# First expert's rows by one-hot products on chip, in a two-layer decoder kernel

## The reference

```python
def hierarchical_moe(h, w_group, b_group, w_router, b_router, w_gate, w_up, w_down):
    hf = h.reshape(b * t, d)                       # 512 x 1024
    grp_p = softmax(hf @ w_group + b_group)        # 4 groups, the best one is taken
    g_sel = argmax(grp_p); g_w = grp_p[g_sel]
    exp_logits = (hf @ w_router + b_router)[g_sel] # 4 experts in the group
    top_p, top_i = top_k(softmax(exp_logits), 2)   # the best two of them
    weights = g_w * top_p / sum(top_p)
    ...
    for e in range(16):
        act = silu(hf @ w_gate[e]) * (hf @ w_up[e])      # 1024 -> 512
        y = y + combine[:, e:e + 1] * (act @ w_down[e])  # 512 -> 1024
    return y
```

## Time and profile before

| | us |
|---|---|
| median of 3 runs | 1290.84 (1289.98 to 1293.81) |
| the profiled execution, its own time | 1289.33 |
| its span in the trace | 1287.6 |
| PE busy (MATMUL) | 1168.3, 91% of the span |
| DVE busy | 912.4, 71% |
| ACT busy | 672.9, 52% |
| POOL busy | 94.5, 7% |
| DMA | 282.52 MB, mean 219 GB/s |

### The profile page before, as it was taken

How to read it: one execution, slowest core, us unless ns; L and a number is a source line. 1 busy time by engine, 2 the same in 40 slices (tenths; PEclk the granted TensorE clock), 3 DMA queues, 4 the chain that set the end, 5 groups by cost and what they waited for, 6 DMA issues and landing times.

```text
span 1287.6 us, 16726 instructions
## 1 busy us (share of the span) xinstructions
PE 1168.3 (91%) x5676; PEld 886.6 (69%) x5676; DVE 912.4 (71%) x1243; ACT 672.9 (52%) x843; POOL 94.5 (7%) x132
## 2 busy tenths in 40 slices
PE   5999879999769999999978999998957999999995
PEld 4776559878647767666646688887855766667663
DVE  4646658555578888888866247646566988888886
ACT  4335641133337787777743241132424787788771
POOL 1120000000010000000030000001001000000003
PEclk9999999899879999999989999999978999999998
DMA  6231110113489999999960240113177999999965
GB/s 221 90 88 66 66 66 1 66 66 132 161 307 354 387 388 385 381 384 391 370 216 1 70 133 18 66 66 131 66 260 258 382 381 380 391 385 384 381 234 206
DMA packets 129645, 282.52 MB, mean 219 GB/s; under 512 B 18976, under 2 KB 19488, under 8 KB 129584
## 3 DMA queue, kind: packets, MB, share of 16 engines
q1 hardware_dynamic: 119680, 246.98, 52.9%
q0 software_dynamic: 6112, 21.76, 5.4%
q10 hardware_dynamic: 3792, 12.98, 2.6%
HBM read 262.83 MB, written 18.87 MB: 219 GB/s over the span
## 4 chain that ended last, share of the span: by engine, by line
PE 57%; DVE 23%; issue 10%; ACT 6%; DMA 2%; POOL 1%; DVEq 1%; ACTq 0%; SPq 0%; POOLq 0%
PE PS L1104 16%; PE PS L1106 16%; PE PS L1105 15%; DVE expert_w_low L1815 9%; PE PS L1208 4%; DVE group_low L1599 2%; ACT weight_high L865 1%; DMA xg<-h_rows,idx 1%; PE PS L1143 1%; DVE xgT_low L1823 1%; DVE score_max L1730 1%; DVE act L1836 1%; DVE x_sb L1534 1%; PE PS L1318 1%; DVE hT_low L1583 1%
## 5 line engine op out<-in xcount | busy, mean ns | idle before, releaser
L1815 DVE TENSOR_TENSOR expert_w_low<-expert_w,weight_high 128x1024 fp32r<-128x1024 f32 x368 | 426.3, 1220 | 74.1 <-ACT weight_high L865 71.8
L865 ACT ACTIVATE weight_high<-expert_w 128x1024 fp32r<-128x1024 f32 x384 | 374.9, 1048 | 65.1 <-PE PS L1106 57.3
L1104 PE MATMUL PS<-weight_high,xgT_high 128*96 128x512 f32 x512 | 204.5, 399 | 7.1 <-DVEq L1825 4.1
L1106 PE MATMUL PS<-weight_high,xgT_low 128*96 128x512 f32 x512 | 203.2, 397 | 0.0
L1105 PE MATMUL PS<-expert_w_low,xgT_high 128*96 128x512 f32 x512 | 202.1, 395 | 0.0
L1104 PE MATMUL PS<-group_high,hT_high 128*128 128x512 f32 x416 | 173.3, 417 | 13.6 <-DVEq L1586 9.2
L1106 PE MATMUL PS<-group_high,hT_low 128*128 128x512 f32 x416 | 166.2, 399 | 0.0
L1105 PE MATMUL PS<-group_low,hT_high 128*128 128x512 f32 x416 | 165.9, 399 | 0.0
L1104 PE MATMUL PS<-weight_high,actT_high 128*96 128x512 f32 x256 | 104.4, 408 | 9.4 <-DVEq L1850 9.0
L1104 PEld LDWEIGHTS PS<-weight_high,xgT_high 128*96 128x96 f32 x512 | 83.3, 163 | 41.8 <-DVEq L1825 4.6
L1599 DVE TENSOR_TENSOR group_low<-group_w,group_high 128x1024 fp32r<-128x1024 f32 x68 | 80.7, 1222 | 43.3 <-ACT group_high L889 39.5
(11 more groups left out here) (248 smaller groups left out, 1436.2 us busy)
## 6 DMA issues: line engine op xcount, KB each, us to landing
expert_w<-in_moe_w_gate SPq DMA_DIRECT2D x32, 2048.0 KB, 13.9
expert_w<-in_moe_w_up SPq DMA_DIRECT2D x32, 2048.0 KB, 14.7
expert_w<-in_moe_w_down SPq DMA_DIRECT2D x32, 2048.0 KB, 13.4
group_w<-in_even_w_in SPq DMA_DIRECT2D x6, 2048.0 KB, 7.8
group_w<-in_odd_w_in SPq DMA_DIRECT2D x6, 2048.0 KB, 7.9
y_rows<-yb ACTq DMA_DIRECT2D x30, 384.0 KB, 6.1
group_w<-in_even_w_out SPq DMA_DIRECT2D x2, 2048.0 KB, 7.9
h_rows<-h SPq DMA_DIRECT2D x8, 512.0 KB, 11.1
```

What stands on the lines that cost most here:

```text
L865: act_(hi, w, ACT.Copy).then_inc(w_hi, 1)
L1104: pe.matmul(out, ah, bh, start=first, stop=False)
L1106: return pe.matmul(out, al, bh, start=False, stop=final)
L1815: tt(lo, w, hi.bitcast(F32), ALU.subtract).then_inc(w_lo, 1)
```

## The change

Expert 0's rows are no longer gathered. DVE makes four more one-hot tiles `oh0` (128 tokens x 96 places, zero where a token doesn't go to expert 0) in the memory of `ein`, and PE multiplies the normalised rows `h`, which are in SBUF, with them: 8 x 4 products of 128x128 by 128x96 in float32, right behind the index product. They give the transposed rows in banks 4 and 5 at once. POOL's first gather takes expert 1's rows. On the other engines the order follows:

- SP: the load of expert 2's gate weights, over `h`, waits for the new product too.
- ACT: `rows_T(0)`, `silu(0)`, half of `high(GATE)`, `rows_T(1)`, the other half, `lastT`.
- PE: `rows_T(1)` is in the middle of expert 0's up product, `lastT` behind it.
- DVE: the copy of `idx` and `nx`, `off` come before `rows_T(0)`, `first_low(1)` behind it as a whole, then q, b, j and the last `ohj`, `low(GATE)` in halves around `rows_T(1)`. `slot` is worked out at the end of block 0 (`slots`), `eid` at the end of block 13 (`further`).

```diff
--- before
+++ after
@@ -365,6 +365,8 @@
             w_of=[2, NT], w_last=[NT], ein=[16, NE],
             ein2=[16, NE], eidf=[16],
         ).items():
+            if name == "ein":
+                oh0 = at("first_onehot", [P, NT, CAP], F32, cursor[0])
             rt[name] = sb("r_" + name, [P] + shape)
         slot = sb("slot", [P, 2, NT], I32)
         assert cursor[0] <= nc.sbuf_usable_end
@@ -413,6 +415,7 @@
         r_gl, r_eg, r_x2, r_e2 = sem("r_groups"), sem("r_exp_groups"), sem("r_second"), sem("r_exp_second")
         M_ready, oh_ready, idx_ready, eid_ready = sem("assigned"), sem("onehots"), sem("idx_ready"), sem("eid_ready")
         idxcol_ready, gathered = sem("idxcol_ready"), sem("gathered")
+        oh0_ready = sem("first_onehot_ready")
         xgT_ready, ex_ready = sem("xgT_ready"), sem("gate_silu_ready")
         xgTh_ready, actTh_ready = sem("xgT_high_ready"), sem("actT_high_ready")
         w_hi, w_lo, w_lo_first = sem("weight_high_ready"), sem("weight_low_ready"), sem("first_low_ready")
@@ -672,6 +675,7 @@
                 expert("up", 1, 4)
                 sp.wait_ge(h_stored, 16 * NT * (l + 1))
                 bk.wait_full(sp, ("route", l))
+                bk.wait_full(sp, ("xgT", l))
                 expert("gate", 2, 5)
 
                 def block_loads(b, par, before="down"):
@@ -791,12 +795,12 @@
                 pool.wait_ge(idx_ready, l + 1)
                 pool.wait_ge(h_stored, 16 * NT * (l + 1))
                 pool.sem_inc(gather_issued, 1)
-                pool.indirect_dma_start(xg[0:CAP, :], None, hbuf[l][:], bass.IndirectOffsetOnAxis(idx[:, 0:1], 0)
+                pool.indirect_dma_start(xg[0:CAP, :], None, hbuf[l][:], bass.IndirectOffsetOnAxis(idx[:, 1:2], 0)
                                         ).then_inc(gathered, 16)
-                with pool.Fori(1, NE) as b:
+                with pool.Fori(2, NE) as b:
 
                     bk.wait_full(pool, ("xgT", l), b - 1)
-                    gather(l, b, idxcol_ready, b + l * (NE - 1), gathered)
+                    gather(l, b, idxcol_ready, b + (l * (NE - 2) - 1), gathered)
                 pool.wait_ge(eid_ready, l + 1)
                 more = pool.value_load(eid[0:1, 15:16], min_val=0, max_val=NX)
                 pool.wait_ge(zero_stored, 16 * NL)
@@ -857,10 +861,10 @@
 
             load_norm(0)
             for l in range(NL):
-                def high(p0, b=0, par=0):
+                def high(p0, b=0, par=0, which=range(SPLITS)):
 
                     wait_loaded(sc, l, p0, b, par)
-                    for part in range(SPLITS):
+                    for part in which:
                         w, hi, _ = parts(l, p0, par, part)
                         act_(hi, w, ACT.Copy).then_inc(w_hi, 1)
 
@@ -1059,14 +1063,14 @@
                         high(LAST)
 
                 rows_T(0, 0)
+                silu(0)
+                high(GATE, which=range(0, 2))
                 rows_T(1, 1)
+                high(GATE, which=range(2, SPLITS))
                 key = ("lastT", l)
                 bk.wait_full(sc, key)
                 link(act_(lastT[:], bank(key)[0:CAP], ACT.Copy))
                 sc.sem_inc(bk.freed(key), 1)
-                bk.wait_full(sc, ("gate", l))
-                high(GATE)
-                silu(0)
                 expert_loop(sc, block_act, link)
                 sc.wait_ge(eid_ready, l + 1)
                 more = sc.value_load(eid[0:1, 15:16], min_val=0, max_val=NX)
@@ -1338,6 +1342,16 @@
                     ins = pe.matmul(bank(key)[0:CAP, 0:NE], ohj[:, k], rt["tok"][:, c, i], start=k == 0, stop=k == 2 * NT - 1)
                 ins.then_inc(bk.filled(key), 1)
 
+                key = ("xgT", l)
+                pe.wait_ge(h_ready, NT * (2 * l + 2))
+                pe.wait_ge(oh0_ready, l + 1)
+                bk.acquire_in_loop(pe, key, 0)
+                for c in range(KD):
+                    for i in range(NT):
+                        ins = pe.matmul(PS[:, 4 + c // 4, c % 4 * CAP:(c % 4 + 1) * CAP], h[:, i, c * P:(c + 1) * P],
+                                        oh0[:, i], start=i == 0, stop=i == NT - 1)
+                ins.then_inc(bk.filled(key), 1)
+
 
                 def wait_low(pos, b, part):
                     if pos < 2:
@@ -1347,7 +1361,7 @@
 
                 def rows_T(b):
                     key = ("xgT", l)
-                    pe.wait_ge(gathered, b * 16 + 16 * (l * NE + 1))
+                    pe.wait_ge(gathered, b * 16 + 16 * l * (NE - 1))
                     bk.acquire_in_loop(pe, key, b)
                     for c in range(KD):
                         ins = pe.transpose(PS[:, 4 + c // 4, c % 4 * CAP:(c % 4 + 1) * CAP],
@@ -1404,17 +1418,15 @@
                     if not last:
                         into("up", b + 1, 1 - par, UP, b, par)
 
-                rows_T(0)
                 pe.wait_ge(xgT_ready, l * NE + 1)
                 into("gate", 0, 0, 0, 0, 0)
-                rows_T(1)
+                into("up", 0, 0, 1, 0, 0, lambda: rows_T(1))
                 key = ("lastT", l)
                 pe.wait_ge(last_ready, l + 1)
                 bk.acquire(pe, key)
                 for i in range(NT):
                     ins = pe.transpose(bank(key)[0:CAP, i * P:(i + 1) * P], ohj[:, i], ident[:])
                 ins.then_inc(bk.filled(key), 1)
-                into("up", 0, 0, 1, 0, 0)
                 expert_loop(pe, block_pe)
                 pe.wait_ge(eid_ready, l + 1)
                 more = pe.value_load(eid[0:1, 15:16], min_val=0, max_val=NX)
@@ -1799,14 +1811,10 @@
                     link(tt(ohj[:, c * NT:(c + 1) * NT], iota_f[:, 0:CAP].unsqueeze(1).broadcast_to(shape),
                             r["rk"][:, c].unsqueeze(2).broadcast_to(shape), ALU.is_equal))
                     ve.sem_inc(oh_ready, 1)
-                first_low(1, range(0, 2))
-                key = ("idx", l)
-                bk.wait_full(ve, key)
-                link(cp(idx[:, 0:NE], bank(key)[0:CAP, 0:NE]))
-                ve.sem_inc(idx_ready, 1)
-                ve.sem_inc(bk.freed(key), 1)
-                first_low(1, range(2, SPLITS))
-
+                for i in range(NT):
+                    ins = ts(oh0[:, i], iota_f[:, 0:CAP], rank[:, i, 0:1], r["M"][:, i, 0:1], ALU.is_equal, ALU.mult)
+                link(ins)
+                ve.sem_inc(oh0_ready, 1)
                 def low(p0, b=0, par=0, which=range(SPLITS)):
 
                     for part in which:
@@ -1836,6 +1844,29 @@
                     link(tt(act[0:CAP], bank(("up", l))[0:CAP], ex[0:CAP], ALU.mult))
                     ve.sem_inc(act_ready, 1)
                     ve.sem_inc(bk.freed(("up", l)), 1)
+
+                def slots():
+
+                    for of, by in (("bc", "b"), ("jc", "j")):
+                        link(tt(r["tA"], r["OH"], r[by].unsqueeze(1).broadcast_to(both), ALU.mult))
+                        link(red(r[of], r["tA"], AX, ALU.add))
+                    link(stt(r["jz"], r["bc"], float(NE - 1), r["jc"], ALU.not_equal, ALU.mult))
+                    link(stt(r["sl"], r["bc"], float(CAP), r["jz"], ALU.mult, ALU.add))
+                    link(cp(slot[:], r["sl"]))
+
+                def further():
+
+                    it8 = iota_f[:, 0:16].unsqueeze(2).broadcast_to([P, 16, NE])
+                    off8 = r["off"].unsqueeze(1).broadcast_to([P, 16, NE])
+                    nx8 = r["nx"].unsqueeze(1).broadcast_to([P, 16, NE])
+                    link(tt(r["ein"], it8, off8, ALU.subtract))
+                    link(tt(r["ein2"], r["ein"], nx8, ALU.is_lt))
+                    link(stt(r["ein2"], r["ein"], 0.0, r["ein2"], ALU.is_ge, ALU.mult))
+                    link(tt(r["ein2"], r["ein2"], iota_f[:, 0:NE].unsqueeze(1).broadcast_to([P, 16, NE]), ALU.mult))
+                    link(red(r["eidf"], r["ein2"], AX, ALU.add))
+                    link(red(r["eidf"][:, 15:16], r["nx"], AX, ALU.add))
+                    link(cp(eid[:], r["eidf"]))
+                    ve.sem_inc(eid_ready, 1)
 
                 def block_ve(b, par):
 
@@ -1860,6 +1891,10 @@
                         times_up(b + 1)
                     if is_int and b == NE - 2:
                         low(LAST, which=range(SPLITS - 1, SPLITS))
+                    if is_int and b == 0:
+                        slots()
+                    if is_int and b == NE - 3:
+                        further()
 
                 ve.wait_ge(r_eg, l + 1)
                 link(red(r["gsum"], r["eg"], AX, ALU.add))
@@ -1870,16 +1905,18 @@
                 link(tt(r["wt"][:, 1], r["wt"][:, 0], r["e2"], ALU.mult))
                 link(tt(r["w_of"], r["OH"][:, :, :, NE - 1], r["wt"], ALU.mult))
                 link(tt(r["w_last"], r["w_of"][:, 0], r["w_of"][:, 1], ALU.add))
-                for i in range(NT):
-                    ins = ts(ohj[:, i], iota_f[:, 0:CAP], rank[:, i, NE - 1:NE], r["M"][:, i, NE - 1:NE], ALU.is_equal, ALU.mult)
-                link(ins)
-                ve.sem_inc(last_ready, 1)
-
```

(35 more changed lines are left out.)

## The result

Over 20 runs of each, the changed kernel takes 1295.07 us in the median (1292.95 to 1297.34) and the one before 1289.20 (1285.17 to 1293.81): ratio 1.0049, 95% interval [1.0041, 1.0057], slower. The one of the changed kernel is 2.2 us above its median, near the top of its 20.

What follows compares the result with a forecast made beforehand. PE was taken as the main bound, with DVE level with it in the loop. Per layer -2.5 + 1.6 + 2.4 = +1.5 us, two layers +3.0: 1292.3 us (1293.9 in the median's terms), range 1285.5 to 1304.0.

Steps and rivals of the forecast that it cites:

- (b): Rival in the expert loop: DVE's moved work is hidden, only the gain stays; -5 us, 1285.8; chance 0.17.
- (c): Rival ahead of block 0: the removed PE wait returns as one for actT_low; +5.8 us, 1296.6; within the forecast's 0.50.
- (a): Rival at the new product: it runs wholly at half clock; together +12 us, 1303; chance 0.28.
- Part 1: Expert 0's rows by product instead of gather: clock rises after 5 us, 9.7 us long, rows ready 1.1 us earlier.
- X: Moment when the product or transposes giving expert 0's rows end; forecast 365.0 instead of 366.14 in layer 0.
- Part 2: From X to the first down product (D0): 22.5 us instead of 23.9, 1.4 gained from the removed wait.
- Part 3: DVE work moved into the loop delays down products: 1.6 us at block 1 for slots, 2.4 at block 14 for further.

Runs made afterwards that it cites:

- e4_two_strips: Changed kernel with the new product in two strips, 64 columns and then 32; 1329.56 us in one execution.
- e7_warm_all: e3_all_ahead plus products nobody reads where PE waits ahead of the rank, index and first gate products; ratio 0.9950 to the kernel before.
- e3_all_ahead: Changed kernel with one-hots in their own memory and q, b, j, last one-hot, slot numbers and further experts under the new product; 1283.18 us, ratio 0.9960.
- e6_further_in_loop: e3_all_ahead with the further experts back at the end of block 13; ratio 1.0022 to the kernel before.
- e1: Kernel before with only the slot numbers moved to the end of block 0 and further experts to that of block 13; 1298.92 us, ratio 1.0094.
- e5: e3_all_ahead with the slot numbers back at the end of block 0; ratio 1.0016 to the kernel before.
- e9: Changed kernel with the moved work split over DVE's waits ahead of low(UP) in blocks 13 and 14 and low(LAST) in 14; 1280.85 us, ratio 0.9937.

## Why the prediction came out as it did

The sign and the range were right, and the measured +5.9 us is twice the forecast's +3.0. That the time lies in the range says little: 1285.5 to 1304.0 also holds rivals (b), (c) and (a). Step by step:

- **Part 1, the product: right.** 9.7 us forecast, 9.89 and 10.48 measured; the clock rose 5.3 us into it in layer 0 and 6.6 in layer 1 (5 forecast), X came 1.1 and 1.0 us earlier (1.1 forecast). Rival (a) didn't come, but in e4_two_strips, with 64 and 32 columns, the clock did stay down. At the low clock a record took 0.213 us there and 0.217 with 96 columns here, so in this range the width hardly matters; e7_warm_all gives (7.36 - 0.27) / 63 = 0.113 at the full one.
- **Part 2, X to D0: mis-sized.** 22.5 us forecast, 23.3 measured, so 0.6 gained instead of 1.4. The failed step is "whether gate 0 runs part of its time at the low clock is hidden below 1.9 us". PE's own path was compared with DVE's, but a third one, gate product, `silu`, `high(GATE)`, `low(GATE)`, was left out; it is 14.1 us from the gate product's end, and that product ran 3.4 us at half clock (7.2 us instead of 5.6). In the trace DVE's own sum is the forecast 22.5, and the 0.83 us that it waits for `high(GATE)` at 377.31 makes it 23.3. e3_all_ahead shows that this chain sets the distance: with DVE relieved it stays. Layer 1 of e6_further_in_loop shows the clock's part: with the gate product at full clock the distance is 21.75. Rival (c) had the mechanism's direction, not its cause; that its +5.8 is nearly the measured +5.9 is luck, since it had the whole gain of 1.4 lost and nothing for the clock.
- **Part 3, the moved work: right in mechanism, short in its second term.** 1.6 forecast and 1.6 / 1.4 measured for `slots`; 2.4 forecast and 2.8 measured for `further` (0.1 above the bounds of 1.8 to 2.7). The forecast took DVE's idle 0.3 off the work's 2.67, but the moved work has a link of its own ahead of it and one behind: 0.24 + 2.82 - 0.30 = 2.76. In layer 1 `slots` costs less because PE had a gap of 0.36 there before. e1, e5, e6 and e9 all show it, and rival (b) falls.
- **Not in the sum: the clock behind the new gaps.** Behind the gaps of 1.69 and 3.21 us in layer 1 the product ran at the low clock for a while, which cost 1.7 and 1.6 us; behind those of layer 0, 1.62 and 3.21, it didn't. Why it is one and not the other is not shown. The earlier trace rows had the pieces for it: a gap, then 0.50.

With the measured terms, 2 x (-1.1 - 0.6 + 1.5 + 2.8) = +5.2 us, and the clock on top in some executions.

## What to carry to other kernels

An engine that is idle 12% of a loop, as DVE is here, has its idle time at certain points: work moved to such points was nearly free (0.2 us for 4.5), the same work elsewhere in the same blocks was paid almost in full. Before moving work, find the wait in that engine's timeline that is as long as the work, and put it right ahead of the instruction that waits. A gap put into TensorE's stream can cost more than its length, since what follows may run at half clock; and a freed wait is worth only the distance to the next chain, which has to be followed over every engine, not only over the two that meet in it.

## What was not expected of the hardware

- TensorE worked 27.5 us without a gap, on float32 records of 128x128 by 64 and 32 columns, and its granted clock stayed at 0.50, the 1.2 GHz level; records with 96 columns saw it rise after 5.3 us (after, layer 0), 6.6 (layer 1) and 3.9 (e6_further_in_loop, layer 1).
- A gap of 1.7 us was enough to find the clock low behind it in layer 1, and not in layer 0 of the same execution, behind 1.62 and even 3.21; nor behind 2.02 in layer 1 of e6_further_in_loop. The length of the gap alone doesn't decide.
- 3.6 us of products that nobody reads, put into a gap of 2 us, neither gained nor lost much: most of what they gave in clock (1.25 us) they took in delay (0.9).
